# Expert weights of a mixture-of-experts step: gate and up loaded as units of one matrix each

## What is computed

```python
def hier_moe(x, rg_w, rg_b, re_w, re_b, w_gate, w_up, w_down):
    ...
    hg = jnp.einsum('nd,edf->nef', xt, w_gate)
    hu = jnp.einsum('nd,edf->nef', xt, w_up)
    a = jax.nn.silu(hg) * hu * combine[:, :, None].astype(x.dtype)
    out = jnp.einsum('nef,efd->nd', a, w_down)
```

## Time and profile before

| what | value |
| --- | --- |
| median of 3 runs | 891.88 us |
| the profiled execution: its time | 891.53 us |
| its span, first to last instruction | 889.6 us |
| mean granted TensorE clock | 0.986 |
| PE busy | 842.9 us (95%) |
| DVE, ACT, POOL busy | 285.9, 264.9, 21.1 us |
| DMA, whole span | 267.85 MB, mean 301 GB/s |
| gate and up loads | 128 DMAs of 1024 KB |
| down loads | 32 DMAs of 2048 KB |

### The profile page before, as it was taken

One profiled execution on the slowest core, in us unless ns is written; L12 is line 12 of the kernel. 1 busy time (PEld: TensorE's weight loads), 2 busy tenths in 40 slices (PEclk: granted clock), 3 DMA queues, 4 the chain that ended last, 5 costly groups with the idle time before them and its releaser, 6 DMA issues.

```text
span 889.6 us, 11190 instructions
## 1 busy us (share of the span) xinstructions
PE 842.9 (95%) x4763; PEld 559.6 (63%) x4763; DVE 285.9 (32%) x387; ACT 264.9 (30%) x471; POOL 21.1 (2%) x37
## 2 busy tenths in 40 slices
PE   6999999999999999997999999999999998898993
PEld 6989999999999999996433333433333333333331
DVE  5374474433764544426001002133004120031203
ACT  5234333322233332314423322432223321222101
POOL 0000000000001000000000000010000100000000
PEclk9999999999999999998999999999999999999997
DMA  9655553565444885487998999999999999999980
GB/s 291 196 144 127 189 175 118 195 206 161 147 142 145 296 283 186 160 324 271 371 423 354 413 421 424 424 423 422 424 425 422 422 424 424 420 424 424 422 346 35
DMA packets 91135, 267.85 MB, mean 301 GB/s; under 512 B 13849, under 2 KB 68943, under 8 KB 69640
## 3 DMA queue, kind: packets, MB, share of 16 engines
q1 hardware_dynamic: 85930, 258.45, 75.6%
q0 software_dynamic: 1920, 5.30, 1.6%
q10 hardware_dynamic: 3238, 3.43, 1.2%
HBM read 263.07 MB, written 11.54 MB: 309 GB/s over the span
## 4 chain that ended last, share of the span: by engine, by line
PE 72%; DMA 16%; DVE 5%; ACT 3%; SPq 3%; issue 1%; POOLq 0%; POOL 0%; ACTq 0%; DVEq 0%
PE ps L1325 17%; PE ps L501 12%; PE ps L503 12%; PE ps L502 12%; PE ps L1359 8%; DMA gu_w<-in_expert_w_up 7%; DMA down_w<-in_expert_w_down 4%; PE ps L1261 3%; SPq L403 3%; DMA raw<-in_w_in 2%; DMA xg<-z_rows,row 1%; ACT xT L1433 1%; DMA out<-xg,sample_row 1%; PE ps L1302 1%; PE ps L528 1%
## 5 line engine op out<-in xcount | busy, mean ns | idle before, releaser
L1325 PE MATMUL ps<-gu_w,xT 128*64 128x512 f32 x1024 | 236.7, 604 | 13.7 <-DMA gu_w<-in_expert_w_up 12.1
L1325 PEld LDWEIGHTS ps<-gu_w,xT 128*64 128x64 f32 x1024 | 73.2, 138 | 142.1 <-issue 135.9
L501 PE MATMUL ps<-xT_hi,w_hi 128*128 128x320 f32 x512 | 159.2, 311 | 0.0
L503 PE MATMUL ps<-xT_hi,w_lo 128*128 128x320 f32 x512 | 158.2, 309 | 0.0
L502 PE MATMUL ps<-xT_lo,w_hi 128*128 128x320 f32 x512 | 158.2, 309 | 0.0
L709 DVE TENSOR_TENSOR w_lo<-raw,w_hi 128x2048 fp32r<-128x2048 f32 x50 | 114.5, 2290 | 135.2 <-ACT w_hi L701 133.9
L701 ACT ACTIVATE w_hi<-raw 128x2048 fp32r<-128x2048 f32 x49 | 93.8, 1915 | 206.1 <-DMA raw<-in_w_in 137.1
L1433 ACT ACTIVATE xT<-ps,gbT 128x64 f32<-128x64 f32 x256 | 82.2, 406 | 153.5 <-PE ps L1261 153.5
L1359 PE MATMUL ps<-down_w,aT 128*64 128x512 f32 x480 | 106.5, 595 | 0.6
L1705 DVE TENSOR_TENSOR a_sb<-ps,a_sb 128x256 f32<-128x256 f32 x16 | 6.8, 425 | 289.6 <-ACT a_sb L1488 289.6
L501 PEld LDWEIGHTS ps<-xT_hi,w_hi 128*128 128x128 f32 x512 | 96.1, 188 | 0.5
(11 more groups left out here) (267 smaller groups left out, 553.8 us busy)
## 6 DMA issues: line engine op xcount, KB each, us to landing
gu_w<-in_expert_w_gate SPq DMA_DIRECT2D x64, 1024.0 KB, 13.9
gu_w<-in_expert_w_up SPq DMA_DIRECT2D x64, 1024.0 KB, 16.4
down_w<-in_expert_w_down SPq DMA_DIRECT2D x32, 2048.0 KB, 24.8
raw<-in_w_in SPq DMA_DIRECT2D x34, 1024.0 KB, 5.4
raw<-in_w_out SPq DMA_DIRECT2D x16, 1024.0 KB, 5.4
tok<-in_x_prompt SPq DMA_DIRECT2D x2, 1024.0 KB, 6.5
z_rows<-z_part ACTq DMA_DIRECT2D x8, 256.0 KB, 5.9
tok<-in_x_sample SPq DMA_DIRECT2D x1, 512.0 KB, 9.8
```

The lines of the kernel that those rows point to most:

```text
L501: pe.matmul(out, wh[:, t, col], hi[:, kt, :], start=(n == 0 and t == 0), stop=False)
L503: last = pe.matmul(out, wl[:, t, col], hi[:, kt, :], start=False, stop=(n == 1 and t == CK - 1))
L1325: last = pe.matmul(ps[C * side:C * (side + 1), GU, :], x, w[:, :, c, FH * side:FH * (side + 1)], start=(j == 0 and c == 0), stop=(j == PAI ...
```

## The change

From unit 5 on a gate/up unit holds one matrix only: units 0 and 1 of an expert are gate and up for the first 1024 rows, units 2 and 3 gate and up for the last 1024. It is one DMA with 16 KB per partition in one piece. Unit 4, the first of expert 1, is issued in two halves as before, but both are gate. Expert 0 keeps the old form.

TensorE therefore needs both units of a pair for each of two steps: it waits for both before the even step and increments `ring_used` by 2 after the odd one. The lower 64 rows of GU now get all 512 features of gate, the upper 64 those of up. So silu and product work on 64 x 512 (`a_sb` is [C, F]), and `turn_a` makes four transposes of 64 x 128. Buffers of `aT` and of small tiles move.

```diff
-    a_sb = at("a_sb", G0 + 19 * KB + 512, [P, FH])
-    aT = at("aT", G0 + 20 * KB + 512, [P, FT // 2, 2, C])
+    a_sb = at("a_sb", G0 + 19 * KB + 512, [C, F])
+    aT = at("aT", MISC, [P, FT // 2, 2, C])
...
-    DMAS = [2 if u < PAIRS else 1 for e, u in ORDER]
+    DMAS = [2 if u < PAIRS and (e == 0 or (e, u) == (1, 0)) else 1 for e, u in ORDER]
...
         src = (gate_v, up_v)[n]
+        if e:
+            src, c = gate_v, 4 * n
...
             if u < PAIRS:
-                for n in range(2):
-                    load_half(sp, i, n)
+                sp.dma_start(gu_w[s][:, :, :].rearrange("p g c -> p (g c)"),
+                             (gate_v, up_v)[u % 2][:, e, u // 2, :, :].rearrange("p c f -> p (c f)"))\
+                  .then_inc(unit_full[s], 16)
...
         def gate_up(e, j):
-            i = AT[e, j]
             pe.wait_ge(xT_ready, FILLS * e + j + 1)
             if e and j == 0:
                 pe.wait_ge(a_ready, e)
-            pe.wait_ge(unit_full[slot(i)], all_in(i))
-            w = gu_w[slot(i)][:, :, :].rearrange("p g (c f) -> p g c f", c=4)
+            if e == 0:
+                i = AT[e, j]
+                pe.wait_ge(unit_full[slot(i)], all_in(i))
+                sides = [gu_w[slot(i)][:, side, :].rearrange("p (c f) -> p c f", c=4) for side in range(2)]
+                used = 1
+            else:
+                at_half = [AT[e, j // 2 * 2 + side] for side in range(2)]
+                if j % 2 == 0:
+                    for i in at_half:
+                        pe.wait_ge(unit_full[slot(i)], all_in(i))
+                sides = [gu_w[slot(i)][:, j % 2, :].rearrange("p (c f) -> p c f", c=4) for i in at_half]
+                used = 2 * (j % 2)
             for c in range(4):
                 x = xT[e % 2][:, j, c, :]
                 for side in range(2):
-                    last = pe.matmul(ps[C * side:C * (side + 1), GU, :], x,
-                                     w[:, :, c, FH * side:FH * (side + 1)],
+                    last = pe.matmul(ps[C * side:C * (side + 1), GU, :], x, sides[side][:, c, :],
                                      start=(j == 0 and c == 0), stop=(j == PAIRS - 1 and c == 3))
-            last.then_inc(ring_used, 1)
+            if used:
+                last.then_inc(ring_used, used)
...
             for c in range(FT // 2):
-                last = pe.transpose(ps[:, bank, P * c:P * (c + 1)], a_sb[:, c:FH:2], ident[:, :])
+                for h in range(2):
+                    last = pe.transpose(ps[:, bank, P * c + C * h:P * c + C * (h + 1)],
+                                        a_sb[:, FH * h + c:FH * (h + 1):2], ident[0:C, 0:C])
...
-            act.activation(a_sb[:, :], ps[:, GU, 0:FH], ACT.Silu).then_inc(silu_ready, 1)
+            act.activation(a_sb[:, :], ps[0:C, GU, :], ACT.Silu).then_inc(silu_ready, 1)
...
-            dve.tensor_tensor(a_sb[:, :], ps[:, GU, FH:F], a_sb[:, :], ALU.mult).then_inc(a_ready, 1)
+            dve.tensor_tensor(a_sb[:, :], ps[C:2 * C, GU, :], a_sb[:, :], ALU.mult).then_inc(a_ready, 1)
```

More of the change, by code:

```diff
@@ L208, in hybrid_trunk_kernel @@
     all_actT = at("all_actT", MISC - 12 * KB, [P, FT, P])
-    small = [MISC + 576]
+    small = [MISC + KB]
     def little(name, shape, dt=FP32):
```

## The result

The changed kernel takes 897.73 us in the median of 6 runs (894.98 to 901.19) against 891.81 us before; the ratio is 1.0082 with a 95% interval of 1.0061 to 1.0103, so it is 5.4 to 9.2 us slower, 7.3 in the middle. The two medians by themselves differ by 5.9 us; the three later groups of executions of the kernel before had medians of 890.0 to 890.5 us, which agrees better with the ratio. The forecast was 897.4 us, 5.9 above its base of 891.5. The profiled execution took 897.43 us, its span is 895.4 us against 889.6.

A forecast was written before the change was run, and what follows sets the result against it. TensorE was taken to set the pace to about 500 us, then the weight stream, with TensorE's work after the last gate/up unit left over; -3.2 + 4.2 + 3.8 + 1.1 = +5.9 on 891.5 gives 897.4 us, range 889.5 to 903.

The forecast's parts named there:

- Larger pieces: Weight loads of experts 1 to 15: 59 units go from 4.96 to about 4.905 us each, -3.2 us.
- Early gaps: Early weight stream: slots released in pairs delay units 15, 20, 21 and 27 by 1.7, 2.1, 3.5, 0.3 us; net +4.2.
- From there the queue is ahead for good: After unit 27's gap at about 516 us: load requests stay ahead, so no further gaps in the stream.
- silu, product, transposes: New 64 x 512 form: silu and product 0.45 us more, felt once at 441.46 us; transposes 0.15 more, hidden except at the end.
- Two steps instead of one at the end: Expert 15: two gate/up steps remain after the last gate/up unit, 19.45 us to the last down pair against 15.64, +3.8.
- Low clock: Expert 15's first pair: TensorE idles 3 us or more for unit 1, then runs at 1.2 GHz, +1.1 us.
- POOL's rows: Gathers at 599 and 707 us: landings 2.5 us later behind longer pieces, TensorE recovered by 834 us, nothing in the sum.
- 8 x 0.31 us: Gather delay: each of 8 pieces per engine waits for one weight piece, whose doubling adds 0.31 us each, 2.5 us.
- late rounds of 29.4 to 29.5 us: Sign that the forecast is right: late expert rounds keep this length; under 29.2 us would show it wrong.
- the prediction's pair of 1.81 (full) and 1.87 (low): TensorE idles in the kernel before: full speed after 1.81 us at 460.49, low clock after 1.87 us in the late stretch.

The follow-up runs named there:

- pieces_only: Kernel before with only the loads of units 5 and up changed to one 16 KB piece per partition, used unit by unit, output meaningless: 0.9972, 2.5 us faster.
- pairs_only: Changed kernel with each one-matrix unit loaded by two DMAs of 8 KB pieces: 1.0109 against the kernel before, 9.7 us slower.
- pair_early: Kernel before, with experts 1 to 3 waiting for units and releasing slots in pairs: 1.0039, 3.5 us slower.
- pair_last: Kernel before, with pairs of waits and releases in expert 15 only: 1.0058, 5.2 us slower.
- after_copy: Changed kernel with ACT copying aT right after the transposes, ahead of silu and the last fill's evictions: 1.0083 against the kernel before.
- best: ends_quiet with ACT copying aT right after the transposes, ahead of silu: 1.0043 against the kernel before, 3.8 us slower.
- ends_quiet: Changed kernel with old units, used one by one, for experts 0 to 3, 7, 8, 11, 12 and 15: 1.0048 against the kernel before.

## Why the prediction was right, and where it was not

The time was right to 0.3 us, and that is luck: the sum left out a cost of 4.0 us, errors in it went against each other, and against the ratio's 7.3 us its +5.9 is 1.4 us low, still inside the interval. The direction and the two largest costs were right for the reasons given.

- *Larger pieces, -3.2 us*: right. 4.90 us a unit at the end, 427 GB/s in pieces_only, and -2.5 us (-3.6 to -1.3) there. Between pairs_only and the changed kernel it is -2.4, within the uncertainty of the two.
- *Early gaps, +4.2 us*: right alone, 3.5 us (2.2 to 4.8) in pair_early. The changed kernel has a gap at each reckoned place, 0.9, 3.0, 3.4 and 0.5 us for 1.7, 2.1, 3.5 and 0.3; less the 3.4 that stood before, that is 4.4 us.
- *"From there the queue is ahead for good"*: wrong. 500 to 600 us is at 408 to 413 GB/s in kernels that turn to pairs at expert 4, and at 418 in the changed kernel, against 424 before. Nor did the stream hold TensorE from 500 us on: the first wait of TensorE for a unit after that in the kernel before is at 728.20 (0.47 us). In between both ran without gaps, TensorE catching up.
- *silu, product, transposes*: this is the step that failed. I put it at 0.45 us once and "elsewhere the down work lies between". Alone it costs 4.0 us (2.5 to 5.4), about half of it through the copy of aT behind a longer silu. It could be seen before: the weight loads of the down step waited 8.9 us for aT even then. It does not add to the pairs in full: pair_early, pair_last and the form alone make 3.5 + 5.2 + 4.0 = 12.7 us, pairs_only, which has all three, 9.7 (7.7 to 11.8). Both delay the same requests; that this is why they don't add is my reading and not shown by a run.
- *Two steps instead of one at the end, +3.8 us*: right, 19.35 us against the 19.45 reckoned.
- *Low clock, +1.1 us*: did not occur in the profiled execution, because TensorE, held up by the form and the gathers, came late and waited 1.49 us, not 3. With a longer wait it does occur, in pair_last and after_copy. The changed kernel had the low clock elsewhere, where the sum had nothing: 0.9 us in the first down step (8.03 for 7.09), 2.5 and 1.7 us in the steps behind the two gathers (6.12 and 5.35 for 3.65).
- *POOL's rows*: each of the two gathers was put at 2.5 us more. A gather lands in 11.9 us for 10.3 in the median, but the scatter in front of it, which the reckoning left out, got longer too (POOL's wait for it 16.42 and 15.30 us for 10.68 and 13.93), and TensorE stood 5.12 and 4.07 us. The rule of the Trainium skill (DMA: Bandwidth & Descriptors, Queues, rings and completion order), that an engine goes round its queues by packets, fits it: in pieces_only nothing but the length of the pieces differs, and the waits appear. That a packet is one piece here, as the 8 x 0.31 us took it, no run shows. That it costs nothing in the end held, if barely: in the profiled execution TensorE had caught up with the stream only at 841.70, and "late rounds of 29.4 to 29.5 us" was wrong.

Put together: pieces_only and pairs_only add up to -2.5 + 9.7 = 7.2 us, and the changed kernel has 7.3. Of the 9.7, the form makes 4.0 alone and the pairs on top of it 5.7. The forecast had 8.0 us for the pairs, 1.1 for a low clock and next to nothing for the form. Against the 4.0 us that were missing stand pairs that cost 2.3 us less on top of the form than reckoned, and the 1.1 us for the clock; with the 0.7 us that the pieces gave less than forecast, 1.3 us are left, from +5.9 to 7.2.

## What to carry to other kernels

A longer DMA piece pays by the per cent that the trace already shows between the two lengths, here 1%; what it asks of the consumer (two buffers held at once, released together) is paid where the queue is shallow and at the end, and both could be read off the timeline before. It also makes the small transfers beside it slower, and there whole chains count, here a scatter and the gather behind it. Before calling work on a side engine hidden, follow the whole order of that engine up to the instruction that the main engine waits for. And where TensorE is made earlier without the data being so, the gained time can return as a longer wait with the low clock behind it.

## What the runs showed of the hardware

**The clock.** Behind every idle of TensorE of 2.32 to 6.16 us that the profiled executions have after 420 us, 16 in all, the next gate/up step was slow, 4.84 to 6.62 us where full clock takes 3.65: 5.35 us after 2.55, 6.62 after 6.16 (granted clock 0.50 there). After a wait of 5.12 us at the third gather the changed kernel ran 6 us at 0.50:

```profile
620.00:626.00 6.00, 5.64 (x16) 2.17 (x18) 5.52 (x4) 1.29 (x4) 0.00 (x0) 0.50 1.01 429
```

For shorter idles the length of the idle alone doesn't decide. At 1.81 us the kernel before kept the full clock in its first down step (7.09 us), and *pieces_only* at the same place with the same idle did not (granted clock 0.52 from 458 to 461 us); *after_copy* kept it after 2.26:

```profile
457.08 0.75 PE L1285 MATMUL ps<-ident,gated 128*128 128x128 f32 x4 [1.81 <-ACT xT L1434]
457.76 8.61 PE L1360 MATMUL ps<-down_w,aT 128*64 128x512 f32 x32
```

```profile
459.80 0.63 PE L1287 MATMUL ps<-ident,gated 128*128 128x128 f32 x4 [2.26 <-ACT xT L1447]
460.36 7.09 PE L1373 MATMUL ps<-down_w,aT 128*64 128x512 f32 x32
```

In *best* the same idle of 2.26 us was followed by a down step of 8.62. After 1.87 the clock was low, after the 2.18 of ends_quiet, above, full. The first step of expert 0, after idles of 1.50 and 1.0 us with little work between them, took 5.35 us before and 3.65 in the changed kernel. So the prediction's pair of 1.81 (full) and 1.87 (low) was no boundary, and a low clock of this kind, worth 1.7 us, comes and goes between executions.

**Small transfers beside long pieces.** A transfer of rows of 8 KB on POOL's queue takes longer beside pieces of 16 KB than beside 8 KB, though the engines move nearly the same bytes per us (427 and 423 GB/s in pieces_only and before). POOL's wait for the scatter ahead of the third and the fourth gather was 10.68 and 13.93 us before and 11.11 and 13.32 in pairs_only, with 8 KB; 15.49 and 15.57 in pieces_only and 16.42 and 15.30 in the changed kernel, with 16 KB. A scatter and the gather behind it held TensorE back by 4.1 to 5.1 us.
